# A two-layer hybrid mixer backbone on one core: projection pieces spread evenly over the scan, and four more weight slots taken before it

## The reference

```python
p = h * (1 + scale) + shift            # adaLN modulation
q.. = p @ w_in                         # one projection, split in 14 parts, four head groups
A: windowed attention with sink, rotary q and k
B: global attention, q and k RMS-normed, then rotary
C: HGRN2 scan, forward and backward:
     f = lb + (1 - lb) * sigmoid(zf);  k = 1 - f
     s = exp(sum log f) * s + k^T v;   o = q s + (masked q k^T) v
D: neighbourhood attention
h = layer_norm(ALPHA * h + gate * (concat(A, B, C, D) @ w_out))
h = layer_norm(ALPHA * h + gate * conv_ffn(h))
```

## Time and profile before

| | us |
|---|---|
| median of 3 runs | 2172.31 (2172.22 to 2176.0) |
| profiled execution, its own time | 2184.93 |
| its span | 2183.1 |
| TensorE busy | 1991.6 (91%) |
| VectorE busy | 1400.0 (64%) |
| GpSimd busy | 998.0 (46%) |
| ScalarE busy | 823.7 (38%) |

### The profile page before, as it was taken

The page is one execution under the profiler, slowest core; times in us unless marked ns, Lnnn a source line. Parts: engine busy times, 40 slices in busy tenths (PEclk is TensorE's granted clock), DMA queues, the critical chain, the costliest instruction groups (busy, mean ns, idle before and its releaser), DMA issues.

```text
span 2183.1 us, 32973 instructions
## 1 busy us (share of the span) xinstructions
PE 1991.6 (91%) x12812; PEld 1701.3 (78%) x12812; DVE 1400.0 (64%) x2711; ACT 823.7 (38%) x1584; POOL 998.0 (46%) x750
## 2 busy tenths in 40 slices
PE   6898988989998899999989998798898988999997
PEld 3678988867787788888878878697886776888786
DVE  3229988775586998999943362897877672222444
ACT  2233524346633222222243343342445633333442
POOL 1236755520154464333353334675624257655543
PEclk7998977999998889999999999887899999999999
DMA  7450100120021332333321121111030112222321
GB/s 319 174 193 21 40 21 20 40 112 2 21 78 39 116 116 100 130 118 116 116 78 68 49 97 59 39 40 39 21 131 2 40 58 77 97 97 97 116 87 68
DMA packets 26938, 177.31 MB, mean 81 GB/s; under 512 B 2720, under 2 KB 3744, under 8 KB 7712
## 3 DMA queue, kind: packets, MB, share of 16 engines
q1 hardware_dynamic: 22544, 157.90, 19.8%
q10 hardware_dynamic: 4240, 17.30, 2.0%
HBM read 171.00 MB, written 4.19 MB: 80 GB/s over the span
## 4 chain that ended last, share of the span: by engine, by line
PE 64%; DVE 16%; POOL 7%; issue 7%; ACT 3%; DMA 2%; DVEq 0%; SPq 0%; POOLq 0%; ACTq 0%
PE PS L1145 22%; PE PS L1070 17%; PE PS L830 5%; PE PS L836 4%; PE PS L1006 3%; PE PS L1031 3%; DVE W L1508 3%; PE PS L990 2%; PE PS L1126 1%; DVE W L1793 1%; DVE U L1694 1%; PE PS L921 1%; POOL WL L2087 1%; PE PS L996 1%; DVE W L1724 1%
## 5 line engine op out<-in xcount | busy, mean ns | idle before, releaser
L1145 PE MATMUL PS<-XH,WS 128*128 128x512 f32 x2016 | 551.8, 361 | 11.8 <-POOL WS L2128 10.8
L1145 PEld LDWEIGHTS PS<-XH,WS 128*128 128x128 f32 x2016 | 365.4, 192 | 69.7 <-POOL WS L2128 7.6
L1145 PE MATMUL PS<-XL,WS 128*128 128x512 f32 x1008 | 362.4, 359 | 0.0
L2128 POOL TENSOR_TENSOR WS<-WR,WS 128x1024 fp32r<-128x1024 f32 x88 | 213.9, 2434 | 321.0 <-ACT WS L1363 320.7
L1432 ACT ACTIVATE W<-PS,PR 128x768 f32<-128x768 f32 (+1 forms) x88 | 78.0, 886 | 451.3 <-PE PS L1145 389.1
L1985 DVE SCALAR_TENSOR_TENSOR W<-PS,PR,W 128x511 f32<-128x511 f32 (+1 forms) x132 | 83.0, 656 | 215.0 <-ACT W L1432 215.0
L1145 PEld LDWEIGHTS PS<-XL,WS 128*128 128x128 f32 x1008 | 194.0, 192 | 27.6
L1508 DVE SCALAR_TENSOR_TENSOR W<-WR,SC,W 128x256 f32<-128x256 f32 x336 | 201.4, 641 | 6.0
L836 PE MATMUL PS<-EU,XH 128*128 128x256 f32 x624 | 194.9, 312 | 6.9 <-issue 6.3
L2087 POOL TENSOR_TENSOR WL<-WR,EU 128x512 fp32r<-128x512 f32 x96 | 126.5, 1339 | 140.7 <-ACT EU L1205 140.6
L836 PE MATMUL PS<-WL,XH 128*128 128x256 f32 x624 | 190.4, 305 | 0.0
(11 more groups left out here) (218 smaller groups left out, 4482.7 us busy)
## 6 DMA issues: line engine op xcount, KB each, us to landing
WR<-in_weights SPq DMA_DIRECT2D x134, 1024.0 KB, 4.8
U<-in_weights SPq DMA_DIRECT2D x10, 1024.0 KB, 6.9
U<-in_bias ACTq DMA_DIRECT2D x2, 1792.0 KB, 10.2
H<-in_x SPq DMA_DIRECT2D x1, 2048.0 KB, 10.7
H<-in_x ACTq DMA_DIRECT2D x1, 2048.0 KB, 15.2
U<-in_ln_rows ACTq DMA_DIRECT2D x2, 1024.0 KB, 4.3
WR<-in_weights SPq DMA_DIRECT2D x4, 512.0 KB, 3.6
kept<-H ACTq DMA_DIRECT2D x4, 512.0 KB, 2.6
```

The costliest lines, as they stand in the source:

```text
L1145: mm = pe.matmul(PS[u.pos][:, lo:hi], w[:, part, k, :], src[:, k, lo:hi], start=(k == 0 and src is xh3 and part == 0), stop=(k == KT - 1 a ...
L2128: pool.tensor_tensor(ws5[:, u.c % 2, 1], half_slot(u), ws5[:, u.c % 2, 0], ALU.subtract).then_inc(w_low, 1)
```

## The change

`ORDER` becomes one order for each layer. In layer 0 it is QC, GC, IC, QB, KVB, FCF, FCB, QA, KVA, VD, QD, KD, and everything up to FCB is an own job: 40 own jobs with mods instead of 28, the 16 mods spread between the jobs from QC to KVB. In layer 1 the order and the own jobs stay.

The jobs beside the scan are cut in four pieces each (a quarter of the matmuls). Each piece gets a unit by the sum of the estimated times of all pieces ahead of it, so that every unit has about the same. In layer 0 they are QA, KVA, VD, QD, KD over units 1 to 24, 2.8 to 4.4 us a unit by the change's own estimates; in layer 1 FCF's latent jobs stay in front of unit 0 and the rest goes over units 0 to 24. The PE queue's waits of a job stand at its first piece; its sum is signalled, and older jobs are transposed, at its last. ScalarE and VectorE take a job at the unit of its last piece. Low and high weight pieces are placed anew; in layer 1 KVA, KVB and KD have all four at one unit.

The roots and rotations of QB and KVB in layer 0 move with them into the own phase of VectorE and GpSimd. The fourth weight place moves within U from column 17920 to 3072.

```diff
-ORDER = (QC, GC, IC, FCF, FCB, QA, KVA, QB, KVB, VD, QD, KD)
+ORDERS = ((QC, GC, IC, QB, KVB, FCF, FCB, QA, KVA, VD, QD, KD),
+          (QC, GC, IC, FCF, FCB, QA, KVA, QB, KVB, VD, QD, KD))
...
-    mixed += gate[:2]
-    back = whole(FCB)
-    rest = [p for s in ORDER[5:] for p in whole(s)]
-    beside = {-2: gate[2:3], -1: gate[3:4], 0: back[:2], 1: back[2:3], 2: back[3:4]}
-    units = 4 * NT
-    first = 3
-    m = units + 1 - first
-    for i in range(m):
-        beside[first + i] = rest[i * len(rest) // m:(i + 1) * len(rest) // m]
-    return mixed, beside
+    if gate == 3:
+        mixed += forget[:2]
+        early, flow = forget[2:], [p for s in order[gate + 1:] for p in whole(s)]
+    else:
+        mixed += forget + whole(FCB)
+        early, flow = [], [p for s in order[gate + 2:] for p in whole(s)]
+    span = lambda p: 5.8 if p[0] == "tok" else 2.9 if p[2] else 5.45
+    total = sum(span(p) for _, p in flow)
+    jobs, at = [], 0.0
+    for i, (key, part) in enumerate(early):
+        jobs.append((key, part, [i - 2] * PIECES))
+    for key, part in flow:
+        steps = [at + span(part) * q / PIECES for q in range(PIECES)]
+        jobs.append((key, part, [int(t / total * UNITS) + 1 for t in steps] if gate != 3
+                     else [int(t / total * (UNITS + 1)) for t in steps]))
+        at += span(part)
+    return mixed, jobs
...
-            late.setdefault(begin + q // 2, []).append((at, q))
+            i = b + 2 if order[at] == QD else b + 1 + (q // 2 if need >= b + 3 else 0)
+            late.setdefault(i, []).append((at, q))
...
-        places = [WR[:, r * SLOT:(r + 1) * SLOT] for r in range(RING)] + [U[:, 17920:17920 + SLOT]]
+        places = [WR[:, r * SLOT:(r + 1) * SLOT] for r in range(RING)] + [U[:, 3072:3072 + SLOT]]
...
+            def project(l, j, piece):
+
+                if piece == 0:
                     if j.freed:
                         pe.wait_ge(job_act, j.freed)
                     pe.wait_ge(in_low, pieces_to(l, j.order, PIECES - 1))
...
+                if j.kind == "tok":
+                    i, ks = piece // 2, range(4 * (piece % 2), 4 * (piece % 2) + 4)
+                else:
+                    i, ks = 0, range(2 * piece, 2 * piece + 2)
+                for k in ks:
+                    for n, (wl, xl) in enumerate(((False, False), (True, False), (False, True))):
+                        mm = job_product(j, i, k, wl, xl, start=(k == 0 and n == 0), stop=(k == KT - 1 and n == 2))
+                if piece < PIECES - 1:
+                    return
+                mm.then_inc(job_sum, 1)
...
-                    projections(l, beside[l, i])
+                    for j, q in pieces_at[l, i]:
+                        project(l, j, q)
...
                     if j.is_e:
                         forget(j)
+                    if j.rope:
+                        rotate(j)
...
-                for n in sorted(splits[l][0]):
-                    for q in range(PIECES):
-                        low_weights(l, splits[l][0][n], q)
+                for n, j in enumerate(own_of[l]):
+                    if n in splits[l][0]:
+                        for q in range(PIECES):
+                            low_weights(l, splits[l][0][n], q)
+                    head_roots([j] if j.kind != "mod" else [])
```

More of the change, by code:

```diff
@@ L44, in slot_parts @@
     return [("tok", p, 0) for p in range(2 + ctx)]
-ORDER = (QC, GC, IC, FCF, FCB, QA, KVA, QB, KVB, VD, QD, KD)
+ORDERS = ((QC, GC, IC, QB, KVB, FCF, FCB, QA, KVA, VD, QD, KD),
+          (QC, GC, IC, FCF, FCB, QA, KVA, QB, KVB, VD, QD, KD))
 PIECES = 4
+UNITS = 4 * NT
 def mixer_jobs(l):
     whole = lambda s: [(("in", l, s, 0), p) for p in slot_parts(l, s)]
-    gate = whole(FCF)
-    own = whole(QC) + whole(GC) + whole(IC)
+    order = ORDERS[l]
+    gate = order.index(FCF)
+    own = [p for s in order[:gate] for p in whole(s)]
+    forget = whole(FCF)
     extra = [(("mod", 0, i, 0), ("mod", i, 0)) for i in range(MOD_FIRST, 24)] if l == 0 else []
@@ L79, in weight_splits @@
+    return mixed, jobs
+def weight_splits(l):
+    own, jobs = mixer_jobs(l)
+    order = ORDERS[l]
+    begin = {}
+    for key, _, at in jobs:
+        begin.setdefault(order.index(key[2]), at[0])
     behind, late = {}, {}
     starts = [n for n, (key, _) in enumerate(own) if key[0] == "in"]
-    for at in range(4):
-        opening = [n for n in starts if own[n][0][2] == ORDER[at]][0] + (at == 0)
+    own_slots = sorted({order.index(own[n][0][2]) for n in starts})
+    for at in own_slots:
+        opening = [n for n in starts if own[n][0][2] == order[at]][0] + (at == 0)
@@ L83, in weight_splits @@
         behind[opening] = at + 1
-    for at in range(5, len(ORDER)):
-        begin = first[at - 1] + (ORDER[at] == QD)
+    for at in range(own_slots[-1] + 2, len(order)):
+        b, need = begin[at - 1], begin[at]
         for q in range(PIECES):
-            late.setdefault(begin + q // 2, []).append((at, q))
+            i = b + 2 if order[at] == QD else b + 1 + (q // 2 if need >= b + 3 else 0)
+            late.setdefault(i, []).append((at, q))
     return behind, late
@@ L104, in uses @@
             if n in behind:
[L105 to L108, removed]
+                u.append(("in", l, ORDERS[l][behind[n]], 0))
+        for i in range(-2, UNITS + 1):
+            u += [("in", l, ORDERS[l][at], 0) for at, _ in late.get(i, [])]
+            u += [key for key, _, at in beside if i in at]
         u += [("out", l, n, g) for n in range(2) for g in range(KT // KDN)]
@@ L266, in raw_piece @@
         def raw_piece(t, l, at, q):
[L268 removed]
+            place = PLAN[SLOT_AT["in", l, ORDERS[l][at], 0]][0]
             return pair(t, place * SLOT + 512 * q)
@@ L436, in hybrid_backbone @@
             own, late = mixer_jobs(l)
-            for when, (key, part) in [(None, p) for p in own] + [(i, p) for i in sorted(late) for p in late[i]]:
+            for key, part, units_at in [(key, part, None) for key, part in own] + late:
                 j = Job()
-                j.l, j.slot, j.key, j.at = l, key[2], key, when
+                j.l, j.slot, j.key, j.units_at = l, key[2], key, units_at
+                j.at = units_at[-1] if units_at else None
                 j.kind, j.a, j.b = part
@@ L499, in hybrid_backbone @@
         units_of = [[u for u in units if u.l == l] for l in range(DEPTH)]
-        beside = {}
+        beside, pieces_at = {}, {}
         for l in range(DEPTH):
@@ L659, in hybrid_backbone @@
             if j.kind != "mod":
-                j.order = ORDER.index(j.slot)
+                j.order = ORDERS[j.l].index(j.slot)
                 first_job.setdefault((j.l, j.order), j)
@@ L882, in projections @@
                     pe.wait_ge(xl_dve, 2 * (KT - POOL_K) * (l + 1))
[L883 to L889, removed]
@@ L1192, in high_weights @@
             def high_weights(l, at, q):
-                place, count, _ = PLAN[SLOT_AT["in", l, ORDER[at], 0]]
+                place, count, _ = PLAN[SLOT_AT["in", l, ORDERS[l][at], 0]]
                 if q == 0:
```

50 lines of the change are left out of this document (25 added, 25 removed).

## The result

The changed kernel takes 2163.81 us (median of 5 runs, 2161.26 to 2167.95), the kernel before beside it 2172.98 (5 runs, 2172.22 to 2176.38). The ratio is 0.995, 95% interval [0.993, 0.9969]: faster by 9 us, where 15 were forecast. The profiled execution took 2167.95 us with a span of 2166.2 and a mean granted clock of 0.942 (before 0.930). The profiled execution of before, 2184.93, was a long one: 35 later executions of that kernel took between 2169.43 and 2184.24.

The account below looks back on a forecast made before the run. The prediction took VectorE and GpSimd shutting each other out as setting the scan's pace. From 2184.9 us it took 11.5 for layer 0 and 4 for layer 1, giving 2169.4, less 12.6 carried over: 2157 us, range 2128 to 2181.

Parts of the forecast that it names:

- The order takes the worst passes away: Layer 0's scan: passes 10 to 15, 15.3 us each beside QB and KVB norm rotations, lose those rotations to the front.
- Own projections end at 212.6: Layer 0 before the scan: 148.2 plus 67.2 of added jobs and transposes, minus 4.8 of weight waits, plus 2.
- The 2 us for late first rotations: Layer 0's own projections: TensorE's transposes may wait for each slot's late first rotation, plus 2 us (0 to 8).
- A bare start of 15.7 us: Layer 0's scan start: chain from last gate to first maps takes 15.7 us, with TensorE standing still for some 15.
- 24 passes at 8.44: Layer 0's scan: 24 passes take 202.6 us, 8.44 each, from base passes of 7.0 and 7.7, rotations and weight pieces.
- passes above 9: Layer 0's scan: passes staying above 9 us were a stated sign that the prediction is wrong.
- Attention at 436.3: Layer 0: pass 24 starts at 430.9, the old tail of 5.4 follows; attention at 436.3 instead of 447.8, 11.5 us won.
- Layer 1 -4: Layer 1's scan: spreading pieces smooths waits, such as 9.6 us before transposes of rotated keys; minus 4 us (-10 to +8).
- 2169.4 in the profile, less 12.6 carried over: Whole kernel: profiled execution forecast at 2169.4 us; its old 12.6 us excess over the median is kept, giving 2157.
- TensorE as pace: Rival for layer 0's scan: VectorE and GpSimd meetings vanish, passes go to 6.8 to 7.6 us, 2117 to 2137; chance 0.15.
- The full pair of engines: Rival for layer 0's scan: VectorE and GpSimd exclude each other, pass 9.4 us, 2180, slower from 9.26 on; chance 0.22.
- Given back: Rival: bare start, half clock and engine meetings eat the saving; passes 8.9 to 9.26 us, 2168 to 2177, no change; chance 0.15.

Follow-up runs that it names:

- order_only: The changed kernel's new layer 0 order, but whole jobs instead of pieces in both layers; 2168.99 us, 0.9964 of the kernel before.
- l0_only: Layer 0 as in the changed kernel, layer 1 with whole jobs at the units of before; 2168.40 us, 0.9962 of the kernel before.
- l1_only: Layer 0 with the order and whole jobs of before, layer 1 with pieces spread as in the changed kernel; 2171.22 us, 0.9976 of the kernel before.
- thin_products: The changed kernel with one product instead of three in every job beside layer 0's scan; 2162.25 us, 0.9941 of the kernel before.
- short_keys: The changed kernel with GpSimd's key multiply made a one-input instruction in both layers, factor 1-f left out; 2134.22 us, 0.9821 of the kernel before.

## Why the prediction was right, and where its terms were off

- **The order takes the worst passes away.** Right. Passes 10 to 15 at 15.3 us are gone, and the new order alone brings the whole gain of layer 0 (order_only 0.9964, l0_only 0.9962).
- **Own projections end at 212.6.** Too late by 7.1; they end at 205.5. The added stretch was 57.3 us instead of 64.4. The 2 us for late first rotations did not occur. The rest is in the 78.2 us that stood there before: by its clock of 0.93 some 14% of it ran at 1.2 GHz, 11 us, of which half is lost. I took off the waits of 4.8 and not the half clock. Afterwards the clock is 0.99. Much of this was a matter of the one execution: in l1_only the same jobs took 74.6 us, from 68.4 to 143.0, at a clock of 0.96.
- **A bare start of 15.7 us.** Right: from 205.7 to 221.02, of which 15.34 is shown as TensorE's wait for GpSimd's keys. It is a loss of the order and can be mended: filled with two jobs, the kernel gains another 6 us.
- **24 passes at 8.44.** This is the term that failed: 9.04 (8.88 in l0_only). It lies outside the forecast's own 7.6 to 8.9, and passes above 9 were one of the signs that I had set for being wrong; the time stayed in its range because other terms made up for it. Passes 0 to 11 took 9.1 each, where the sum, 7.0 + 0.85 of rotation + 0.67 of pieces, is 8.5; passes 12 to 20 took 9.0, where 7.7 + 0.67 is 8.4. In the first half the price of a rotation was wrong. These are the groups of the rotations of QA and KVA, from 221.1 to 410.9:

```profile
L1685 DVE TENSOR_TENSOR U<-U,CN 128x256 f32<-128x256 f32 (+1 forms) x8 | 7.5, 934 | 0.0
L1691 DVE TENSOR_TENSOR U<-U,CN 128x128 f32<-128x128 f32 (+1 forms) x16 | 5.5, 384 | 0.0
L1678 DVE COPY U<-U 128x512 f32<-128x512 f32 x2 | 3.9, 1957 | 0.0
L1697 DVE TENSOR_TENSOR U<-U 128x256 f32<-128x256 f32 (+1 forms) x8 | 2.5, 355 | 0.1
```

  They took VectorE 19.4 us for the 10.2 in the sum, and these 9 us are more than the 6.5 by which the twelve passes were too long. In the second half there are no rotations, and the blocking inside the scan and the subtractions was larger, 1.28 and 0.46 us on average against 0.80 and 0.35 in the first. Over all, VectorE's clean 5.78, 1.5 of blocking inside the scan and the subtractions, 0.9 of waiting before L1765 (18.6 us in 21 passes) and 0.9 of rotations are 9.1. I had the blocking in the rows, and took it that a regular beat would not need more of it than passes 4 to 9 had; nor did the beat become regular. By the exclusive lock of the Trainium skill (SBUF — State Buffer, section "SBUF: two separate sides") taken for whole instructions it would have been 9.4; the 8.88 and 9.04 of two traces lie between that and my sum.
- **Attention at 436.3.** It came at 438.0. The front was 7.2 us too early, 21 passes were 12.6 too long, and what follows was 3.6 shorter than the three passes and the old tail in the sum (27.1 for 30.7). Errors that cancelled: luck, and no credit to the sum. Nor was 447.8 a sound start: in l1_only, with the layer 0 of before, attention begins at 439.4. Layer 0 brought some 8 us by the medians, where I summed 11.5.
- **Layer 1 -4.** -2.2 in this trace; the stretch of 249.9 is 247.0 in l1_only, whose layer 1 is the same. Inside the range. The wait before the transposes of rotated keys was to shrink from 9.6; it is 14.1:

```profile
PE PS L929 <- ACT U L1300: 8.8, 2, 4.6
PE PS L929 <- ACT U L1302: 5.3, 2, 2.9
```

  I named the wrong place. What the profile shows beside the gain is a higher clock, 0.89 for 0.84, with TensorE's busy time down from 216.80 to 207.95 us for as many matmuls.
- **2169.4 in the profile, less 12.6 carried over.** The profiled execution took 2167.95, within 1.5 of the sum for it. The median is only 4.1 below that. The 12.6 of before was a property of that execution, and much of it lay in the very stage that changes: l1_only's execution, only 0.7 above its median, has before's order in layer 0 and reaches attention 8.4 us earlier, 5.2 of them already at the first scan of VectorE (147.98 for 153.18). The FFN of layer 0, whose code is the same, took 408.3 us at a clock of 0.95 and after the change 401.8 at 0.97, but that doesn't explain it: from attention to the end of the FFN l1_only takes 655.3 us and before 655.9. So the offset makes the forecast 8.5 us too low and the other terms make it 1.5 too high, which leaves the 6.8 between 2157.0 and 2163.8 (but for rounding).
- **The rivals.** TensorE as pace is refuted by thin_products. The full pair of engines names the right mechanism: the two-input work of VectorE and GpSimd blocks each other, and short_keys shows that the pace hangs on it in both layers. Its size, 1.5 us a pass inside the scan and the subtractions and 0.4 in the rotations, stayed short of the 9.26 from which the kernel would have been slower. "Given back" has the bare start right (some 6 us of the gain) and its passes of 8.9 to 9.26 hold the 9.04; with 9.04 in the prediction's own formula the time is 2171, no change. That the kernel came out some 7 us faster than that matches the front that was early by 7, not the passes.

## What to carry to other kernels

Before a chain of engines is lined up behind the last job of a stage, look for work that doesn't depend on that chain: two jobs moved into the hole were worth as much as two thirds of the whole change. What dealing work out evenly is worth depends on what stands around it, and has to be measured in its place: here it was worth nothing with the bare start, 16 us with the filled one, some 5 in layer 1, and it cost 10 in layer 0 with the old order. And the difference of one profiled execution to its median can lie in the very stage that the change touches, as here: forecast a ratio of medians, and take the stage's time from more than one execution.

## What was not expected of the hardware

A GpSimd instruction with one input from SBUF did not hold VectorE's two-input instructions up. In short_keys a tensor_scalar over 128x1024 ran from 252.42 for 2.77 us, and VectorE's products of 256 columns inside it took 0.52 and 0.41 us, against 2.03 for one that met the two-input keys before; the two-input weight pieces right behind it did block, 1.87 and 1.51 us. The Trainium skill (SBUF — State Buffer, section "SBUF: two separate sides") lets any GpSimd instruction that reads SBUF exclude a VectorE instruction with two inputs; this trace doesn't agree for the one-input form. The other way round it does block: GpSimd's one-input clamp takes 1.37 us behind VectorE's L1765 and 0.53 without it. And the one-input form is the slower one on GpSimd itself: 2.82 us on average for 128x1024 against 2.42 for the product of two tensors, the first operand and the size being the same (medians 2.78 and 2.37). VectorE's two-input instructions inside it didn't lengthen it either: it takes 2.77 at 252.42, around four of their groups.
